# Splitting latent-attention queries and keys into rounded high and low parts, with the low parts formed by GpSimd

## What is computed

```python
def mla_attention(h, w_in, q_norm, kv_norm, w_q_up, w_kv_up, w_out, cos, sin):
    q_lat, kv_lat, k_pe = jnp.split(h @ w_in, [B_Q_LORA, B_Q_LORA + B_KV_LORA], axis=-1)
    q = (rms_norm(q_lat, q_norm) @ w_q_up).reshape(b, s, B_HEADS, B_NOPE + B_ROPE)
    kv = (rms_norm(kv_lat, kv_norm) @ w_kv_up).reshape(b, s, B_HEADS, B_NOPE + B_V)
    ...
    for i in range(s // Q_BLOCK):
        logits = (einsum(q_nope[:, q0:q1], k_nope[:, :q1])
                  + einsum(q_pe[:, q0:q1], k_pe[:, :q1])) * scale
        logits = jnp.where(mask[None, None], logits, -jnp.inf)
        probs = jax.nn.softmax(logits, axis=-1)
        outs.append(einsum(probs, v[:, :q1]))
    return concatenate(outs, axis=1).reshape(b, s, B_HEADS * B_V) @ w_out
```

## Time and profile before

| | us |
|---|---|
| median of 3 runs | 1807.49 |
| lowest, highest | 1806.69, 1807.75 |
| profiled execution | 1805.97 |
| its span | 1804.2 |

### The profile page before, as it was taken

The page is one execution under the profiler, slowest core; times in us unless marked ns, Lnnn a source line. Parts: engine busy times, 40 slices in busy tenths (PEclk is TensorE's granted clock), DMA queues, the critical chain, the costliest instruction groups (busy, mean ns, idle before and its releaser), DMA issues.

```text
span 1804.2 us, 23133 instructions
## 1 busy us (share of the span) xinstructions
PE 1787.3 (99%) x8521; PEld 1465.4 (81%) x8521; DVE 918.9 (51%) x1393; ACT 621.2 (34%) x1054; POOL 140.7 (8%) x119
## 2 busy tenths in 40 slices
PE   8999999999999999999999999999999999999998
PEld 6888888887788888888888888888867788888887
DVE  5543443468654334445543443456897544344375
ACT  5322222347543223223332231233566443122222
POOL 0100100011011001010110010100000011010010
PEclk9999999999999999999999999999999999999999
DMA  6433333233333333333333333234112333333321
GB/s 180 119 93 94 103 95 90 85 110 90 87 104 95 97 95 100 94 88 98 106 93 99 94 98 95 88 95 123 27 41 62 94 94 116 93 95 103 93 94 58
DMA packets 316435, 170.50 MB, mean 95 GB/s; under 512 B 13330, under 2 KB 311503, under 8 KB 316367
## 3 DMA queue, kind: packets, MB, share of 16 engines
q1 hardware_dynamic: 314656, 167.07, 31.7%
q10 hardware_dynamic: 1710, 2.53, 0.5%
HBM read 163.03 MB, written 2.10 MB: 92 GB/s over the span
## 4 chain that ended last, share of the span: by engine, by line
PE 94%; DVE 2%; issue 1%; ACT 1%; DMA 1%; SPq 0%; POOL 0%; DVEq 0%; ACTq 0%; POOLq 0%
PE bank L1190 29%; PE bank L1191 29%; PE bank L1192 29%; PE bank L1447 2%; PE bank L1470 1%; PE bank L1459 1%; DMA w_raw<-ffn_gu 1%; ACT w_hi L569 0%; PE bank L1358 0%; PE bank L1328 0%; PE bank L1204 0%; DMA m_q<-work 0%; PE bank L1343 0%; DVE w_lo L794 0%; DVE xT L863 0%
## 5 line engine op out<-in xcount | busy, mean ns | idle before, releaser
L1190 PE MATMUL bank<-h_hi,w_hi 128*128 128x512 f32 x1520 | 594.5, 391 | 0.2 <-DVE h_lo L822 0.2
L1192 PE MATMUL bank<-h_hi,w_lo 128*128 128x512 f32 x1520 | 591.9, 389 | 0.0
L1191 PE MATMUL bank<-h_lo,w_hi 128*128 128x512 f32 x1520 | 591.7, 389 | 0.0
L794 DVE TENSOR_TENSOR w_lo<-w_raw,w_hi 128x1024 fp32r<-128x1024 f32 (+2 forms) x316 | 391.5, 1240 | 309.8 <-ACT w_hi L569 301.1
L569 ACT ACTIVATE w_hi<-w_raw 128x1024 fp32r<-128x1024 f32 (+2 forms) x316 | 317.0, 1004 | 287.6 <-PE bank L1192 271.1
L1190 PEld LDWEIGHTS bank<-h_hi,w_hi 128*128 128x128 f32 x1520 | 285.4, 188 | 59.8 <-DVE h_lo L822 0.6
L1192 PEld LDWEIGHTS bank<-h_hi,w_lo 128*128 128x128 f32 x1520 | 285.4, 188 | 59.7
L1191 PEld LDWEIGHTS bank<-h_lo,w_hi 128*128 128x128 f32 x1520 | 285.5, 188 | 58.1
L1190 PE MATMUL bank<-y_hi,w_hi 128*128 128x512 f32 x784 | 306.3, 391 | 0.7 <-DVE w_lo L794 0.7
L1192 PE MATMUL bank<-y_hi,w_lo 128*128 128x512 f32 x784 | 305.3, 389 | 0.0
L1191 PE MATMUL bank<-y_lo,w_hi 128*128 128x512 f32 x784 | 305.2, 389 | 0.0
(11 more groups left out here) (160 smaller groups left out, 1053.4 us busy)
## 6 DMA issues: line engine op xcount, KB each, us to landing
w_raw<-ffn_gu SPq DMA_DIRECT2D x176, 512.0 KB, 3.7
w_raw<-ffn_d SPq DMA_DIRECT2D x70, 512.0 KB, 3.9
w_raw<-ffn_d SPq DMA_DIRECT2D x24, 384.0 KB, 3.3
w_raw<-a_in SPq DMA_DIRECT2D x10, 512.0 KB, 3.9
w_raw<-a_out SPq DMA_DIRECT2D x8, 512.0 KB, 4.2
w_raw<-b_out SPq DMA_DIRECT2D x8, 512.0 KB, 3.7
w_raw<-b_in SPq DMA_DIRECT2D x5, 512.0 KB, 3.8
w_raw<-b_qup SPq DMA_DIRECT2D x16, 144.0 KB, 2.3
```

The costliest lines, as they stand in the source:

```text
L794: last = v.tensor_tensor(w_lo[:, sl, 0:k, 0:m], w_raw[:, sl, 0:k, 0:m], w_hi[:, sl, 0:k, 0:m].bitcast(F32), ALU.subtract)
L1190: t.matmul(b[:, :], wh, hi[:, c, :], start=c == 0, stop=False)
L1191: t.matmul(b[:, :], wh, lo[:, c, :], start=False, stop=False)
L1192: last = t.matmul(b[:, :], wl, hi[:, c, :], start=False, stop=c == k - 1)
```

## The change

Queries and keys of each head are split in two parts of fp32r, and `scores` makes three products of them in place of one in float32.

- ScalarE gets `head_high(h)`: after the scaled query of head h is there it copies the head's key (128 x 512) and query (128 x 512) into `k_hi` and `q_hi`. Its place is behind `high` and ahead of `exponentials(h-1)`, and for head 0 ahead of the loop.
- GpSimd gets `head_low(h)`: two subtractions of 128 x 512 that make `k_lo`, then `q_lo`. It also takes over `low` for the head weights of heads 4 to 15. Its order is `head_low(0)`, and then for each h `low` of the block four heads ahead and `head_low(h+1)`.
- VectorE loses these `low` calls for twelve heads and keeps those of the output projection (at h = 12 to 14), ahead of which it now waits for the split before it.
- TensorE's `scores(h)` waits for `k_split` and `q_split` in place of the query's `evac_done`, and issues 12 matrix products in place of 4. The wait for the shared rotary key goes from TensorE to ScalarE.

The new buffers lie over others that are idle then.

```diff
+            def head_low(h):
+                pool.wait_ge(khi_done, h + 1)
+                g.tensor_tensor(k_lo[:, h % 2, :], kt_b[h % 2][:, h // 2, :], k_hi[:, h % 2, :].bitcast(F32),
+                                ALU.subtract).then_inc(k_split, 1)
+                pool.wait_ge(qhi_done, h + 1)
+                g.tensor_tensor(q_lo[:, h % 2, :], qt_b[:, h % 2, :], q_hi[:, h % 2, :].bitcast(F32),
+                                ALU.subtract).then_inc(q_split, 1)
+            def low(n):
+                k, sl = KQ, n % SLOTS
+                pool.wait_ge(split_done, n + SLOTS)
+                pool.wait_ge(hi_done, n + 1)
+                g.tensor_tensor(w_lo[:, sl, 0:k, 0:QD], w_raw[:, sl, 0:k, 0:QD],
+                                w_hi[:, sl, 0:k, 0:QD].bitcast(F32), ALU.subtract)
+                g.tensor_tensor(behind(w_lo, sl, k), exchanged(w_raw, sl, k),
+                                behind(w_hi, sl, k).bitcast(F32), ALU.subtract).then_inc(split_done, 1)
+            head_low(0)
+            for h in range(HEADS):
+                if h + 1 + AHEAD < HEADS:
+                    low(n + h + 1 + AHEAD)
+                if h + 1 < HEADS:
+                    head_low(h + 1)
...
+            def head_high(h):
+                if h == 0:
+                    act.wait_ge(kpe_in, 64)
+                act.wait_ge(evac_done, n + FIRST + h + 1)
+                a.activation(k_hi[:, h % 2, :], kt_b[h % 2][:, h // 2, :], ACT.Copy).then_inc(khi_done, 1)
+                a.activation(q_hi[:, h % 2, :], qt_b[:, h % 2, :], ACT.Copy).then_inc(qhi_done, 1)
             high(n + AHEAD)
+            head_high(0)
             for h in range(HEADS):
                 if h + 1 < HEADS:
                     high(n + h + 1 + AHEAD)
+                    head_high(h + 1)
                 exponentials(h)
...
                 maxima(h)
-                if h + 1 < HEADS:
+                if HEADS <= h + 1 + AHEAD < HEADS + AHEAD:
+                    dve.wait_ge(split_done, n + h + 1 + AHEAD + SLOTS)
                     low(n + h + 1 + AHEAD)
                 probabilities(h)
...
             def scores(h):
-                pe.wait_ge(evac_done, q_0 + h + FIRST + 1)
+                pe.wait_ge(k_split, h + 1)
+                pe.wait_ge(q_split, h + 1)
...
-                        last = t.matmul(SC[b][:, S_AT[i]:S_AT[i] + (i + 1) * P],
-                                        qt_b[:, h % 2, i * P:(i + 1) * P],
-                                        kt_b[h % 2][:, h // 2, 0:(i + 1) * P], start=True, stop=True)
+                        t.matmul(to, qh[:, q], kh[:, k], start=True, stop=False)
+                        t.matmul(to, ql[:, q], kh[:, k], start=False, stop=False)
+                        last = t.matmul(to, qh[:, q], kl[:, k], start=False, stop=True)
```

More of the change, by code:

```diff
@@ L194, in build @@
         w_lo = sb("w_lo", [P, SLOTS, KD, P], F32R)
+        with ExitStack() as keys:
+            k_hi = keys.enter_context(nc.sbuf_tensor("k_hi", [P, 2, S], F32R))
+            k_lo = keys.enter_context(nc.sbuf_tensor("k_lo", [P, 2, S], F32R))
         xg = sb("xg", [P, 2, S])
@@ L209, in build @@
         sm = sb("sm", [P, 2, 6, TT])
+        with ExitStack() as queries:
+            queries.enter_context(nc.sbuf_tensor("below", [P, 20 * P + 3 * S + TT * S], F32))
+            q_hi = queries.enter_context(nc.sbuf_tensor("q_hi", [P, 2, S], F32R))
+            q_lo = queries.enter_context(nc.sbuf_tensor("q_lo", [P, 2, S], F32R))
         work = sb("work", [P, 8 * S + 3 * (CHUNK + S) + 3 * S])
@@ L315, in build @@
         kpe_in = sem("kpe_in")
+        qhi_done = sem("qhi_done")
+        khi_done = sem("khi_done")
+        q_split = sem("q_split")
+        k_split = sem("k_split")
         skv_ready = sem("skv_ready")
@@ L535, in _ @@
             power(M_Q)
-            n += 6 + KV_BLOCKS + HEADS
+            n += 6 + KV_BLOCKS
+            def head_low(h):
[19 more added lines that the diff above has]
+                    head_low(h + 1)
+            n += HEADS
             power(M_F)
@@ L1438, in scores @@
             def scores(h):
-                pe.wait_ge(evac_done, q_0 + h + FIRST + 1)
+                pe.wait_ge(k_split, h + 1)
+                pe.wait_ge(q_split, h + 1)
+                qh, ql, kh, kl = (z[:, h % 2, :] for z in (q_hi, q_lo, k_hi, k_lo))
                 for b, tiles in enumerate(S_BANKS):
@@ L1442, in scores @@
                         pe.wait_ge(v_evac, 2 * KV_BLOCKS)
-                        pe.wait_ge(kpe_in, 64)
                     else:
@@ L1446, in scores @@
                     for i in tiles:
-                        last = t.matmul(SC[b][:, S_AT[i]:S_AT[i] + (i + 1) * P],
-                                        qt_b[:, h % 2, i * P:(i + 1) * P],
-                                        kt_b[h % 2][:, h // 2, 0:(i + 1) * P], start=True, stop=True)
+                        to, q, k = SC[b][:, S_AT[i]:S_AT[i] + (i + 1) * P], slice(i * P, (i + 1) * P), slice(0, (i + 1) * P)
+                        t.matmul(to, qh[:, q], kh[:, k], start=True, stop=False)
+                        t.matmul(to, ql[:, q], kh[:, k], start=False, stop=False)
+                        last = t.matmul(to, qh[:, q], kl[:, k], start=False, stop=True)
                     last.then_inc(s_full, 1)
```

## The result

The changed kernel takes 1810.83 us (median of 14 runs, 1809.01 to 1812.39) against 1806.77 (14 runs, 1806.05 to 1807.75) for the kernel before in the same comparison: +4.1 us, a ratio of 1.0023 with a 95% interval of 1.0016 to 1.0030. The profiled execution has a span of 1808.1 at the same granted clock, 0.999.

A forecast was written before the change was run, and what follows sets the result against it. TensorE, busy 99% of the span, was taken as the bound, VectorE a close second. Start +2.2, heads 0 to 3 +1.4, pairs +1.5, heads 12 to 14 +1.2 made +6.3, rounded to +7: 1814.5 us, range 1806.5 to 1821.

The forecast's parts named there:

- main case: Head loop: GpSimd's k_lo holds up VectorE's two-element negative in each head; +7 us, 1814.5; chance 0.43.
- TensorE's saving: Scores: 12 fp32r products take 1.91 us in place of 2.16, 0.25 less per head, 12.6 a pair.
- GpSimd's prices: GpSimd's splits: 1.30 us per 128 x 512 subtraction, 1.2 for low of a weight block.
- The start: Loop start: first scores wait for GpSimd's splits, 3.4 us after scaled_q(0) ends; +2.2 us.
- Who waits for GpSimd: VectorE: two-SBUF-input and double-rate instructions, including the two-element negative, wait out GpSimd's whole instruction; one-element forms pass.
- Heads 0 to 3: Heads without outputs, paced by VectorE: 6.23 us in place of 5.89, +0.34 each, +1.4.
- Heads 12 to 14: VectorE keeps a 1024-column low there: together 23.5 us against TensorE's 22.3, +1.2.
- The pairs from head 4 on: Five pairs: 0 by sum, plus 0.3 each for GpSimd meeting one scaling; +1.5 us (0 to 2.5).
- +0.87 a head: VectorE's two-element negative, due at T + 1.02, waits for k_lo and ends at T + 2.06, not T + 1.19.
- Rival 1: Head loop: the negative isn't blocked, TensorE's 12.6 sets the pairs; +1 us (-3 to +4.5), about 1808.5; chance 0.36.
- Rival 2: Head loop: all three forms of the negative are blocked; +11.5 to +17 us, about 1822; chance 0.16.
- Rival 3: Scores get no cheaper, 128-column product at 0.216 us; +3 to +4.5 under Rival 1; chance 0.10, within Rival 1's.

The follow-up runs named there:

- e1: Changed kernel with GpSimd's two subtractions per head cut to 2 columns in place of 512: 1802.94 us, 7.9 below the changed kernel.
- e2: Changed kernel with the two-element scaled negative of bank 0 as two one-element instructions: 1806.25 us, 4.6 below the changed kernel.
- e3: Changed kernel with the weights' low parts back on VectorE, GpSimd keeping queries' and keys': 1816.77 us, 5.9 above the changed kernel.
- e6: e2 with keys of heads 0 and 1 split ahead of the loop and head 0's query low part on VectorE: 1804.78 us, 1.5 below e2.
- e4: Kernel before plus three unused 128 x 512 GpSimd subtractions per head, started by scaled_q: 1815.90 us, +9.0.
- e7: e6 with every later key split one step earlier on ScalarE and GpSimd: 1804.62 us, no different from e6.

## Why the prediction came out as it did

Forecast was +7 (1814.5) with a range from 1806.5 to 1821; measured +4.1 over the kernel before of the same comparison, or 1810.83. The direction and the mechanism of the main case hold. One term was too high by 2.4, the sum of 6.3 was rounded up by 0.7, and two terms came out near their numbers partly by luck. The 1814.5 also started from 1807.49, where the kernel before gave 1806.77 in the comparison.

- **TensorE's saving** (0.25 a head, 12.6 a pair): right, 12.58 in e1 and e2. The price that no row had, the 128-column fp32r product, was put at 0.11; the changed kernel's starts (timeline) give 0.11 to 0.12:

```profile
1341.67 0.28 PE L1499 MATMUL bank<-k_hi,q_lo 128*128 128x128 f32 x1
...
1341.79 0.27 PE L1500 MATMUL bank<-k_lo,q_hi 128*128 128x128 f32 x1
1341.90 0.39 PE L1498 MATMUL bank<-k_hi,q_hi 128*128 128x384 f32 x1
```

- **VectorE's relief** (0.53 a head) and **ScalarE's fit**: right; e3 gives the first back, and the second shows in ScalarE's 10.78 a pair and in e1.
- **GpSimd's prices**: 1.29 for 128 x 512, and 0.82 + 0.39 = 1.2 for a weight block, as put.
- **The start** (+2.2): +2.26. e6 took most of it away, and the time followed.
- **Who waits for GpSimd**: the reading of the double mode from the slope of 0.52 ns and from 0.17 against 0.15 was right about who waits in all three cases: two elements wait, one does not (e2), the scalings do. The double mode itself is inferred from the times, not seen in a trace. The Trainium skill's rule ("SBUF — State Buffer", section "Who interferes with whom"), that a VectorE instruction in a two-port mode and a GpSimd one exclude each other, is borne out here by L1155 too (0.29 became 0.98 to 1.01 where it met `q_lo`), which no row of before showed. What the Trainium skill's "Vector Engine (DVE) Microarchitecture Reference", section 5.1, says of two elements of one source in SBUF, that they run in that mode, agrees with the negative's 1.04.
- **Heads 0 to 3** (+1.4): +1.15, near it partly by luck. The sum added 0.34 to each of four heads at 5.89. But only the last distance was 5.89 before: the scores of heads 0 to 4 lay 4.24, 5.33, 5.69 and 5.89 apart, and now lie 4.01, 5.89, 6.99 and 5.42 apart, two longer and two shorter.
- **Heads 12 to 14** (+1.2): +0.98, again partly by luck. The negative waited in heads 13 and 14 but not in head 12 (0.17); there the weight split of 1024 columns, for which the sum had no wait, met `q_lo` and took 1.99 in place of 1.22.
- **The pairs from head 4 on** (+1.5, 0 to 2.5): wrong, -0.9 over four pairs. The step that failed is "+0.87 a head". It took `k_lo` to start at T + 0.73 in every head (T is the end of `scaled_q`). In the odd heads it does (0.74 to 0.82). In the even heads from 2 to 10 ScalarE comes late out of `transposed`, not to its copies but to `high` of the weights ahead of them: in head 8 `high` ends at 1344.64, 0.25 behind T, where in head 9 it ended 0.57 ahead of it. GpSimd's weight split waits for it and stands ahead of `k_lo`, which starts at T + 1.50 (T is 1344.39 here):

```profile
1344.33 0.31 ACT L609 ACTIVATE w_hi<-w_raw 128x96 fp32r<-128x96 f32 x1
...
1344.50 0.65 ACT L792 ACTIVATE k_hi<-kt 128x512 fp32r<-128x512 f32 x1
...
1344.78 0.80 POOL L563 TENSOR_TENSOR w_lo<-w_raw,w_hi 128x288 fp32r<-128x288 f32 x1 [3.34 <-ACT w_hi L609]
...
1345.41 0.20 DVE L1145 TENSOR_SCALAR sm<-sm 128x2 f32<-128x2 f32 x1
1345.54 0.39 POOL L565 TENSOR_TENSOR w_lo<-w_raw,w_hi 128x96 fp32r<-128x96 f32 x1
...
1345.89 1.28 POOL L552 TENSOR_TENSOR k_lo<-kt,k_hi 128x512 fp32r<-128x512 f32 x1
```

  The negative meets only the tail of the weight split's first instruction (0.20) and is done before `k_lo`, and `q_lo`, now late, meets a scaling instead, for 0.70 (1.32 against 0.62). So a pair has one wait of 0.87 and one of 0.70, not two of 0.87 and a third on top: 11.34 + 0.87 + 0.70 = 12.91, against 12.94 measured. That is 0.16 under the pair of before, where the sum had 0.3 over it and its sign was to be 13.1 to 13.6. The first of the four pairs gained 0.41, since before it took 13.35. I had added the scaling's wait to the negative's, and in no head do both wait.
- **TensorE's idle time**, forecast at some 10 released by `q_lo`, shows as 5.2: 2.1 before the first scores and 3.1 for `q_lo`, in three heads. The rest of its waiting does not show in its records, and the chain of waits names VectorE, not `q_lo`, as what sets the pace.
- **Rival 1** is not what happened, but e2 makes it come true by one edit, at 0.6 below the kernel before (no difference by its interval) and within its band of -3 to +4.5. **Rival 2** is excluded by the one-element form's 0.154. **Rival 3** is excluded by e1's pairs.

## What to carry to other kernels

Moving elementwise work to an idle GpSimd is not free for VectorE: what VectorE runs meanwhile with two SBUF inputs (the weight split of 288 columns in e4), or with one where it runs at double rate (L1155, and L1145 of two elements), waits until the GpSimd instruction ends, even if it has two elements to do. Price such a move by laying GpSimd's instructions over VectorE's timeline, with each start shifted by the waits before it (a negative that waits lets the scaling pass), and look first for tiny double-rate instructions on the path; here, one of two elements split in two of one gave back 4.6 us. Splits that feed the first step of a pipeline also need an early start, since no earlier work covers them.

## What was not expected of the hardware

- The fp32r products with their own 128-column weights cost, start to start, 0.11 to 0.12 at 128 columns and 0.12 at 256 (0.17 at 384 and 0.23 at 512, all in e1), so the narrow one is hardly cheaper than one of twice its width.
- A subtraction on GpSimd took 0.20 at 2 columns (e1), 0.39 at 96, 0.82 at 288 and 1.29 at 512: about 0.2 fixed and 2.1 ns a column.
- A VectorE scaling (TENSOR_SCALAR) of one SBUF element passes beside GpSimd, one of two elements waits: 0.151 against up to 1.11. It is not the two elements alone: the reciprocal of two SBUF elements (L1151) ran in the midst of `q_lo` in five heads at 0.15 to 0.16.
- GpSimd waits too when it comes second. In the changed kernel its split of 288 columns at 1298.95, begun during a scaling of 512 columns (1298.79 to 1299.28), took 0.99 in place of 0.82, and in e7 a `k_lo` begun during such a scaling took 1.51 in place of 1.29.
